# Reordering the first microseconds of a two-block transformer kernel: transfers, split weights and the first 96 products

## What is computed

```python
def rms_norm(x, g):
    y = xf * lax.rsqrt(jnp.mean(xf * xf, axis=-1, keepdims=True) + EPS)
    return (y * g).astype(x.dtype)

def swiglu(h, w_gate, w_up, w_down):
    return (jax.nn.silu(h @ w_gate) * (h @ w_up)) @ w_down

x = x + 0.5 * swiglu(rms_norm(x, ffn1_norm), ffn1_w_gate, ffn1_w_up, ffn1_w_down)
```

## Time and profile before

| | us |
|---|---|
| median of 3 runs | 2334.64 (2334.54 to 2336.59) |
| the profiled execution, device time | 2337.08 |
| its span, first to last instruction | 2335.3 |
| PE busy | 2234.3 (96% of the span) |
| DVE busy | 952.2 |
| ACT busy | 843.8 |
| POOL busy | 909.2 |
| mean granted TensorE clock | 0.97 of full speed |

### The profile page before, as it was taken

One profiled execution on the slowest core, in us unless ns is written; L12 is line 12 of the kernel. 1 busy time (PEld: TensorE's weight loads), 2 busy tenths in 40 slices (PEclk: granted clock), 3 DMA queues, 4 the chain that ended last, 5 costly groups with the idle time before them and its releaser, 6 DMA issues.

```text
span 2335.3 us, 29338 instructions
## 1 busy us (share of the span) xinstructions
PE 2234.3 (96%) x10442; PEld 1832.5 (78%) x10442; DVE 952.2 (41%) x1449; ACT 843.8 (36%) x1244; POOL 909.2 (39%) x383
## 2 busy tenths in 40 slices
PE   6999999999999999999998889999999879999999
PEld 5888887788887788888876668888888768888887
DVE  4222222354534532222225665555322884555500
ACT  4233222422333332323333434444322553444421
POOL 3444444332354244444432123444543104444453
PEclk9999999899999999999998879999999889999999
DMA  4333333212243223333331112332333102333332
GB/s 145 102 93 97 101 108 106 63 60 68 82 127 108 63 90 99 90 100 106 101 128 46 37 46 90 93 105 90 108 108 127 37 19 81 99 90 99 99 108 81
DMA packets 58686, 210.26 MB, mean 90 GB/s; under 512 B 6640, under 2 KB 7408, under 8 KB 58224
## 3 DMA queue, kind: packets, MB, share of 16 engines
q1 hardware_dynamic: 56736, 202.07, 28.2%
q10 hardware_dynamic: 1872, 7.10, 0.8%
HBM read 207.05 MB, written 2.10 MB: 90 GB/s over the span
## 4 chain that ended last, share of the span: by engine, by line
PE 74%; issue 13%; POOL 6%; DVE 5%; ACT 1%; POOLq 0%; DVEq 0%; ACTq 0%
PE psum L208 22%; PE psum L209 22%; PE psum L210 22%; POOL w_lo L182 6%; PE psum L226 1%; PE psum L227 1%; PE psum L228 1%; DVE swa_s L2116 1%; PE psum L1197 1%; PE psum L1172 1%; PE psum L756 1%; DVE swa_most L2122 1%; DVE swa_s L2134 1%; PE psum L1555 0%; PE psum L1954 0%
## 5 line engine op out<-in xcount | busy, mean ns | idle before, releaser
L182 POOL TENSOR_TENSOR w_lo<-w_raw,w_hi 128x1024 fp32r<-128x1024 f32 x379 | 909.0, 2405 | 1407.2 <-ACT w_hi L170 1407.2
L208 PE MATMUL psum<-x_hi,w_hi 128*128 128x512 f32 x1808 | 721.1, 399 | 32.4 <-DMA block_ones<-in_squares 15.3
L209 PE MATMUL psum<-x_lo,w_hi 128*128 128x512 f32 x1808 | 714.1, 395 | 0.0
L210 PE MATMUL psum<-x_hi,w_lo 128*128 128x512 f32 x1808 | 713.4, 395 | 0.0
L170 ACT ACTIVATE w_hi<-w_raw 128x1024 fp32r<-128x1024 f32 x379 | 394.4, 1054 | 617.2 <-PE psum L210 578.1
L208 PEld LDWEIGHTS psum<-x_hi,w_hi 128*128 128x128 f32 x1808 | 345.4, 191 | 110.4 <-DMA block_ones<-in_squares 15.3
L210 PEld LDWEIGHTS psum<-x_hi,w_lo 128*128 128x128 f32 x1808 | 345.1, 191 | 74.5
L209 PEld LDWEIGHTS psum<-x_lo,w_hi 128*128 128x128 f32 x1808 | 345.8, 191 | 72.3 <-issue 0.2
L248 DVE SCALAR_TENSOR_TENSOR x<-psum,x 128x512 f32<-128x512 f32 x64 | 44.3, 692 | 389.8 <-PE psum L210 389.8
L208 PE MATMUL psum<-ffn_hidden_hi,w_hi 128*128 128x512 f32 x352 | 136.9, 389 | 0.0
L209 PE MATMUL psum<-ffn_hidden_lo,w_hi 128*128 128x512 f32 x352 | 136.9, 389 | 0.0
(11 more groups left out here) (309 smaller groups left out, 2599.6 us busy)
## 6 DMA issues: line engine op xcount, KB each, us to landing
w_raw<-in_stream SPq DMA_DIRECT2D x379, 512.0 KB, 3.6
swa_bias<-in_swa_bias ACTq DMA_DIRECT2D x1, 2048.0 KB, 10.7
out<-x SPq DMA_DIRECT2D x8, 256.0 KB, 4.7
ab_bias<-in_ab_bias ACTq DMA_DIRECT2D x1, 1792.0 KB, 7.1
x<-in_x_in SPq DMA_DIRECT2D x4, 256.0 KB, 5.1
x<-in_x_in ACTq DMA_DIRECT2D x4, 256.0 KB, 6.8
xattn_mem<-in_mem ACTq DMA_DIRECT2D x1, 1024.0 KB, 4.8
mix_k_turned<-in_gate_w ACTq DMA_DIRECT2D x1, 256.0 KB, 3.6
```

The costliest lines, as they stand in the source:

```text
L182: pool.tensor_tensor(self.w_lo[:, split, :], self.w_raw[:, raw, :], self.w_hi[:, split, :].bitcast(F32), ALU.subtract).then_inc(self.w_lo_ ...
L208: pe.matmul(out, w_hi, hi[:, k0 + j, :], start=first and j == order[0], stop=False)
L209: pe.matmul(out, w_hi, lo[:, k0 + j, :], start=False, stop=False)
L210: mm = pe.matmul(out, w_lo, hi[:, k0 + j, :], start=False, stop=last and j == order[-1])
```

## The change

- SP issues its four x tiles and the four weight units in turns: x 0, unit 0, x 2, unit 1, x 4, unit 2, x 6, unit 3, then the constant squares. ACT's queue is unchanged.
- DVE makes the low parts of units 0 to 3 (`Chip.vector_lower`), each behind x_lo of tiles 1, 3, 5, 7. POOL begins with unit 4, once these four are done.
- ACT first makes all x_hi, with the high part of unit m // 2 behind x_hi of each odd m (unit 3 now among them), and then the eight squares. DVE makes all x_lo and the four low parts, and then the eight sums.
- PE no longer waits for the constants at its start, but ahead of the stat. It takes units 0 to 3 tile by tile side by side, in four banks (`opening`): units 0 and 1 with x tiles 0 to 3, both with 4 and 5, unit 2 with 0 to 5, units 0, 1 and 2 with 6 and 7, then the stat, unit 3 with 0 to 3, the spread, unit 3 with 4 to 7. `units_done` rises with the last group of each unit.
- ACT makes a small copy of `eps` into `root_col` before it waits for the columns; DVE sets `eps` first for it.
- `Out` gets a list of 8 banks and arguments for parts that no caller uses here; its instructions stay as they were.

```diff
@@ Chip
+    def vector_lower(self, u):
+        dve = self.nc.vector
+        dve.wait_ge(self.w_hi_ready, u + 1)
+        dve.tensor_tensor(self.w_lo[:, u, :], self.w_raw[:, u, :], self.w_hi[:, u, :].bitcast(F32), ALU.subtract
+                          ).then_inc(self.w_lo_ready, 1)
@@ Ffn.tensor
+        def opening():
+            there = lambda k: pe.wait_ge(c.x_lo_ready, DT * self.norm.split_n + k + 1)
+            for n, tiles in ((0, (0, 1, 2, 3)), (1, (0, 1, 2, 3)), (0, (4, 5)), (1, (4, 5)), (2, (0, 1, 2, 3, 4, 5)),
+                             (0, (6, 7)), (1, (6, 7)), (2, (6, 7)), (3, (0, 1, 2, 3)), (3, (4, 5, 6, 7))):
+                if n == 3 and tiles[0] == 0:
+                    pe.wait_ge(c.consts_landed, 48)
+                    self.norm.tensor_stat()
+                elif n == 3:
+                    self.norm.tensor_spread()
+                c.products(c.bank(n), u0 + n, u0 + n, c.x_hi, c.x_lo, order=tiles, first=tiles[0] == 0,
+                           last=tiles[-1] == DT - 1, done=tiles[-1] == DT - 1, wait_tile=there if n == 0 else None)
+        opening() if self.opens else pair(0, True)
@@ Ffn.scalar, gated
-            c.split_ahead(f * 2 + u0, place)
+            if not (self.opens and isinstance(f, int) and f == 0):
+                c.split_ahead(f * 2 + u0, place)
@@ sync
             for m in range(0, DT, 2):
                 sp.dma_start(c.x[:, m, :], x_in[m]).then_inc(c.x_landed[m], 16)
-            for u in range(RAW_SLOTS):
-                sp.dma_start(c.w_raw[:, u, :], stream[u]).then_inc(c.w_landed[u], 16)
+                sp.dma_start(c.w_raw[:, m // 2, :], stream[m // 2]).then_inc(c.w_landed[m // 2], 16)
@@ gpsimd
-            c.split_lo_program(pool)
+            pool.wait_ge(c.w_lo_ready, RAW_SLOTS)
+            first = RAW_SLOTS
+            c.lower_stretch(pool, first, c.units)
@@ scalar
+            act.wait_ge(c.pads_zero, 2)
+            act.activation(c.root_col[:, 0:1], c.eps[:], ACT.Copy, scale=1.0)
             act.wait_ge(c.columns_landed, 16)
             for m in range(DT):
-                norms[0].scalar_tile(m)
-                if m % 2 == 1 and m // 2 < AHEAD:
+                norms[0].scalar_upper(m)
+                if m % 2 == 1:
                     c.split_hi(m // 2, m // 2)
+            for m in range(DT):
+                norms[0].scalar_square(m)
@@ vector
             for m in range(DT):
                 dve.wait_ge(c.x_landed[m], 16)
                 norms[0].vector_update(m)
-                norms[0].vector_split(m)
+                norms[0].vector_lower(m)
+                if m % 2 == 1:
+                    c.vector_lower(m // 2)
+            for m in range(DT):
+                norms[0].vector_sum(m)
@@ tensor
-            pe.wait_ge(c.consts_landed, 48)
```

More of the change, by code:

```diff
@@ L175, in split_ahead, with lower, lower_stretch @@
         self.split_hi(u + AHEAD, place + AHEAD)
[L177 to L186, removed]
+    def lower(self, pool, u, place):
+        pool.wait_ge(self.w_hi_ready, u + 1)
+        raw, split = place % RAW_SLOTS, place % SPLIT_SLOTS
+        pool.tensor_tensor(self.w_lo[:, split, :], self.w_raw[:, raw, :],
+                           self.w_hi[:, split, :].bitcast(F32), ALU.subtract).then_inc(self.w_lo_ready, 1)
+    def vector_lower(self, u):
[3 more added lines that the diff above has]
+                          ).then_inc(self.w_lo_ready, 1)
+    def lower_stretch(self, pool, first, end):
+        turns = end // RAW_SLOTS
+        with pool.Fori(first // RAW_SLOTS, turns) as turn:
             for slot in range(RAW_SLOTS):
-                lower(turn * RAW_SLOTS + slot, slot)
-        for u in range(turns * RAW_SLOTS, self.units):
-            lower(u, u)
+                self.lower(pool, turn * RAW_SLOTS + slot, slot)
+        for u in range(turns * RAW_SLOTS, end):
+            self.lower(pool, u, u)
     def products(self, out, u, place, hi, lo, first=True, last=True, tiles=UNIT_TILES, k0=0, width=P,
-                 x_needed=None, order=None, wait_tile=None):
+                 x_needed=None, order=None, wait_tile=None, done=True):
         pe = self.nc.tensor
@@ L256, in vector_split, with vector_lower, vector_sum @@
     def vector_split(self, m):
+        if self.gain:
+            self.vector_lower(m)
+            self.vector_sum(m)
+    def vector_lower(self, m):
         c, dve = self.c, self.c.nc.vector
[L259 to L269, removed]
+        dve.wait_ge(c.x_hi_ready, self.hi_done(m))
+        dve.scalar_tensor_tensor(c.x_lo[:, m, :], c.x[:, m, :], self.gain_column(m), c.x_hi[:, m, :].bitcast(F32),
+                                 ALU.mult, ALU.subtract).then_inc(c.x_lo_ready, 1)
+    def vector_sum(self, m):
+        c, dve = self.c, self.c.nc.vector
+        dve.wait_ge(c.x_squared, self.done(m))
+        if m == 0:
+            own(dve, dve.tensor_copy(c.square_sum[:], c.square[:, 0, :]), c.x_summed, self.done(m))
+        else:
+            own(dve, dve.tensor_tensor(c.square_sum[:], c.square_sum[:], c.square[:, m % 2, :], ALU.add),
+                c.x_summed, self.done(m))
     def hi_done(self, m):
@@ L584, with __init__, wait_tile, tensor_part @@
 class Out:
-    def __init__(self, chip, u0, following, hi, lo, order, waits, banks=(4, 5, 6, 7)):
+    def __init__(self, chip, u0, following, hi, lo, order, waits, banks=(4, 5, 6, 7, 4, 5, 6, 7)):
         self.c, self.u0, self.next, self.hi, self.lo = chip, u0, following, hi, lo
         self.order, self.waits, self.banks = order, waits, banks
[L592 to L602, removed]
+    def wait_tile(self, k):
+        self.c.nc.tensor.wait_ge(*self.waits[k])
+    def tensor_part(self, m, tiles):
+        c = self.c
+        c.products(c.bank(self.banks[m]), self.u0 + m, self.u0 + m, self.hi, self.lo, order=tiles, last=False,
+                   wait_tile=self.wait_tile if m == 0 else None, done=False)
+    def tensor(self, pe, parts=0, early=()):
         c = self.c
         for m in range(DT):
-            c.split_ahead(self.u0 + m, self.u0 + m)
+            before = [n for n in range(m) if self.banks[n] == self.banks[m]]
+            if before:
+                pe.wait_ge(c.x_updated, self.next.done(before[-1]))
+            order = [k for k in self.order if m >= parts or k not in early]
+            c.products(c.bank(self.banks[m]), self.u0 + m, self.u0 + m, self.hi, self.lo, order=order,
+                       first=m >= parts, wait_tile=self.wait_tile if m == 0 else None)
+    def scalar(self, act, split_first=True):
+        c = self.c
+        for m in range(DT):
+            if m > 0 or split_first:
+                c.split_ahead(self.u0 + m, self.u0 + m)
             if m > 0:
@@ L612, in vector @@
         for m in range(DT):
-            self.next.vector_update(m, 1.0, c.bank(self.banks[m % len(self.banks)]), self.u0 + m + 1)
+            self.next.vector_update(m, 1.0, c.bank(self.banks[m]), self.u0 + m + 1)
             self.next.vector_split(m)
```

27 lines of the change are left out of this document (16 added, 11 removed).

## The result

The changed kernel took 2317.35 us (median of 5 runs, 2314.44 to 2320.56) against 2334.64 before: ratio 0.9929, 95% interval 0.9915 to 0.9943. Forecast were 2318.4 and a range of 2316.0 to 2322.5. The profiled execution was the slowest of the five, 2320.56 with a span of 2318.8, for which the prediction gave 2320.9 and 2319.1.

The account below looks back on a forecast made before the run. PE was taken to be bound in its opening: 15.3 us before its first product, then 12.3 us of waits and lower clock. Unit 4 at 34.35 instead of 50.55 gives 2334.64 - 16.2 = 2318.4 us, range 2316.0 to 2322.5.

Parts of the forecast that it names:

- The start: PE's first product in the opening: at 9.85 instead of 15.27 us, once unit 0's low part is ready at 9.8.
- the other bound: Unit 0's transfer on SP's queue: at the later, faster rate it lands at 6.4 us, and PE starts at 9.2.
- the sum: Whole forecast: unit 4 at 34.35 instead of 50.55, 16.2 us gained; its ACT times put x_hi 1 at about 6.15.
- DVE's low parts: Units 0 to 3: 1.25 us each on DVE against POOL's 2.35; three x_lo slowed by POOL save 3 x 1.55.
- Feeding: PE behind its start in the opening: parts always ready before PE asks, narrowest margin 1.1 us at unit 1.
- The nop: The nop of tile m + 1 was assumed to go up while x_lo of tile m or a low part still runs.
- rival 1: In the opening, the nop waits for the running instruction; gain 14.1 us, time 2320.5; chance 0.12.
- The low level: TensorE's 1.2 GHz pace at PE's start: same slow first 3.15 us as before, 7 products, some 1.5 us lost.
- Rival 2: In the opening the clock rises later, after 8.8 us instead of 3.15, costing 2.8 us; time 2321.2; chance 0.12.
- rival 5: PE never gets the higher clock level in the opening; 2337.1, or 2346.7 if low through units 4 and 5; chance 0.06.
- Behind the opening: After units 0 to 3: stat at 27.7, ending 28.5; unit 4's low part covered by 1.9 us, unit 5's by 0.8.
- Rival 3: Units 4 and 5: the covers of 1.9 and 0.8 us fail, costing one 1.55 us; time 2320; chance 0.05.

Follow-up runs that it names:

- e3: Changed kernel, but SP issues the four x tiles first and then the four weight units; median 8.3 us above the changed kernel's, unit 4 at 38.23.
- e2: Changed kernel, but POOL makes the low parts of units 0 to 3 again; unit 4 moved by 1.4 us, no median given in the text.
- e12: The changed kernel unaltered, run again for a second trace; 2316.12 us, unit 4 at 34.39.
- e5: Kernel before, with only PE's side-by-side order of units 0 to 3 added; ratio 0.9979, unit 4 at 48.75.
- e7: Changed kernel with squares and sums again between the parts of x and units one after another; unit 4 moved by 8.4 us, median 6.5 us slower than expected.
- e6: Kernel before, but PE waits for the constants only ahead of its first stat; ratio 1.0002.
- e1: Changed kernel, but PE takes units 0 to 3 one after another; unit 4 moved by 0.0 us, no median given in the text.
- e4: Changed kernel, but squares and sums stand between the parts of x as before; unit 4 at 35.98, no median given in the text.
- e9: Changed kernel plus 24 products of zeros on PE before its first true product; 2317.49 us, unit 4 at 33.00.
- e8: Changed kernel plus 16 products of zeros on PE before its first true product; median 3.7 us slower than expected.
- e10: Changed kernel plus 21 products of zeros, with unit 0's high and low parts ahead of x tile 1's; 2316.68 us, unit 4 at 32.63.

## Why the prediction was right, point by point

**The start.** Forecast 9.85, measured 9.61 and 9.54. The assumption that the n-th kilobyte of SP's queue lands when it did put unit 0 at 7.4; issued at 1.19, it took 5.1 us to land and was there at 6.3, the other bound. But x tile 1 came later: issued at 1.19 on ACT's queue it took 5.4 instead of 4.8, and its x_hi started at 6.63 instead of the 6.15 of the sum. The transfers issued at 1.19, SP's second and ACT's second:

```profile
w_raw<-in_stream SPq DMA_DIRECT2D x1, 512.0 KB, 5.1
x<-in_x_in ACTq DMA_DIRECT2D x1, 256.0 KB, 5.4
```

Unit 0 was 1.1 us earlier than the sum had it, and taking ACT's tiles as unchanged was wrong by 0.6 us. That PE started within 0.3 us of the forecast is in part the luck of two errors that nearly met. e3 shows the price of the order itself: 3.0 us of start.

**DVE's low parts.** 1.23 against 1.25. The end of the meetings of DVE and POOL was right as a fact. As e2 shows, its price to PE was a start 1.0 us later and 1.0 us for one wait, and not the 3 x 1.55 us that DVE lost before.

**Feeding.** No wait behind the start, as forecast; the margin at unit 1 was real (its low part ended at 12.15, PE asked at 14.87, so 2.7 us instead of 1.1, of which the slow products gave 1). The nop ran ahead, so rival 1 fell. By the rule of the Trainium skill, page "PSUM — Partial Sum Buffer", section "Engine vs sequencer instructions", it should, and the row at 8.40 agrees: 1.16 us before the low part ahead of it ended.

**The low level.** This is the term that was mis-sized. I gave it the 3.15 us of before, 7 products. The eighth was half slow there, so that by the table's measure it was 3.50 us and 1.7 us lost. In the changed kernel it lasted 5.26: 12 products, 2.5 us lost instead of the 1.5 of the sum. Over all traces in which PE's first true product was its first and no wait broke in, it lasted from 3.45 (e12) to 6.1 us (e5), and 5.26 and 3.45 for the same kernel. Rival 2 was thus partly true, at a third of its price. The clock did not fall again in the opening: the granted clock is 1.00 from 14.87 to 379.20. So rival 5 fell. The Trainium skill's case of short idles at changes of bank (page "TensorE: Matmul & The Clock Gate", section "A second HAM failure mode: psum-queue depth-cycling") is not what happens here: there are nine changes of bank up to unit 4, no idle time of PE at any of them, and 0.2275 us a product from the rise on, but for the stat and the spread.

**Behind the opening.** Stat at 28.51 (27.7 forecast, late by the low level), unit 5's high part at 36.34, ready with 1 us of cover. Rival 3 fell.

**The sum.** 16.2 us forecast for unit 4, 15.17 measured in this trace and 16.16 in the second. In the first trace the error of 1.03 us is: start 0.24 early, low level 1.0 more, and 23.24 instead of 23.0 for the rest, because the product behind the stat and the one behind the spread each take 0.1 us longer, which the earlier trace rows showed (0.49 and 0.48 us). In the second unit 4 came at 34.39 where the sum said 34.35, by errors that cancel: start 0.31 early, low level 0.1 and the rest 0.2 more. The span moved by 16.5 because the four other stages were 1.3 shorter. The median's closeness to the forecast, 1.05 us, is in part luck: those stages vary by more from run to run.

**What the prediction left out.** It priced each part against the kernel before and did not ask what the parts are worth to each other. e5 to e7 answer it: alone in the old kernel the side-by-side order gives 1.8 us and the removed wait nothing. Undone alone in the new one, and with the slow products taken off as above, the order costs nothing, the squares 1.0 (0.9 of it the start), DVE's low parts 2.0 and the order of the transfers 3.0. The 15.2 us come from two conditions, an early start, for which unit 0 must come early and PE must not wait for the constants, and parts that never make PE wait. The latter can be had in two ways, and the change has both.

## What to carry to other kernels

The longest wait of a profile can be worth nothing by itself (e6: 15.3 us shown, 0.0 gained) and still have to go before other parts of a change can work: find what ends second, third and last behind it. A change made of parts that cover for each other has to be taken apart in pairs: e1 and e4 alone say that neither matters, e7 says that one of them must stay. Where a few us are at stake in a run of 2300, a fixed landmark in the trace (here unit 4) tells what the medians can't, once the part of it that changes from one execution to the next (here the slow products) has been taken off.

## What the runs showed of the hardware

The level of TensorE's clock at the start is a cost of its own, and its length differs from one execution to the next, 3.45 us (e12) to 6.1 us (e5) of work before the rise. Products of zeros raised it (e9), a pause of 0.75 us did not lose it, one of 2.04 did (e8). The column of the granted clock reads 1.00 before the first rise (first row), while products start every 0.43 us there and every 0.2275 us behind it.

In the fourteen traces, whose code is the same behind the opening, token mixing took 247.2 to 252.3 us, cross attention 180.7 to 182.4, differential attention 230.4 to 235.0 and window attention 191.2 to 196.0, together 851.0 to 861.9, and the three full feed-forward stages were constant to 0.1 us (362.0, 360.5, 357.4). The stages in which PE never stops are constant, and those with pauses are not, with PE's own busy time 234.5 to 239.6 in token mixing for the same 1229 recorded products, at a mean granted clock of 0.97 and 0.95. That the fall and rise of the clock around PE's pauses makes these differences fits the rows, but no run here tested it. It sets the limit of what the medians can show: e9 and e10 bring unit 4 forward by 1.4 to 2.7 us, and whether they are faster than the changed kernel stays open.
